# The first norm of a transformer step in four K quarters, each followed by that quarter of three column blocks of the first FFN

## The reference

```
mod = silu(cond) @ ada_w + ada_b           # nine vectors of 2048: shift, scale, gate for each of three norms
h   = rms_norm(x, norm_w) * (1 + scale) + shift
g,u = split(h @ wi)                        # wi is 2048 x 11264, wo is 5632 x 2048
x   = x + 0.5 * gate * ((silu(g) * u) @ wo)
```

## Time and profile before

| | |
|---|---|
| median of three runs | 2425.38 us |
| the profiled execution: its span | 2427.3 us (the page gives no other time of it) |
| PE busy | 2315.6 us, 95% |
| DVE, ACT busy | 1249.6 us, 931.9 us |
| HBM read | 543.73 MB, 225 GB/s over the span |

### The profile page before, as it was taken

One profiled execution on the slowest core, in us unless ns is written; L12 is line 12 of the kernel. 1 busy time (PEld: TensorE's weight loads), 2 busy tenths in 40 slices (PEclk: granted clock), 3 DMA queues, 4 the chain that ended last, 5 costly groups with the idle time before them and its releaser, 6 DMA issues.

```text
span 2427.3 us, 29221 instructions
## 1 busy us (share of the span) xinstructions
PE 2315.6 (95%) x11108; PEld 1798.5 (74%) x11108; DVE 1249.6 (51%) x1289; ACT 931.9 (38%) x1083; POOL 59.9 (2%) x57
## 2 busy tenths in 40 slices
PE   5699999999999998999977999998999999999998
PEld 0277777777777776777766888787888888888886
DVE  1154455554555547444457455455455555555557
ACT  0253333333333334433445344345434444444442
POOL 0000000000000000000040000000000000000000
PEclk7699999999999998999989999999999999999999
DMA  9969788787787875789611555655555555555553
GB/s 367 330 215 323 253 285 284 253 310 264 280 289 251 304 272 191 277 297 321 231 50 42 185 193 181 202 196 175 186 196 190 190 194 190 189 190 189 191 190 112
DMA packets 273183, 547.86 MB, mean 226 GB/s; under 512 B 9022, under 2 KB 9190, under 8 KB 272880
## 3 DMA queue, kind: packets, MB, share of 16 engines
q1 hardware_dynamic: 193936, 386.36, 46.8%
q10 hardware_dynamic: 76176, 151.15, 17.2%
q0 software_dynamic: 3024, 9.71, 1.4%
HBM read 543.73 MB, written 3.46 MB: 225 GB/s over the span
## 4 chain that ended last, share of the span: by engine, by line
PE 91%; DMA 4%; DVE 3%; ACT 1%; issue 0%; ACTq 0%; DVEq 0%
PE ps L525 27%; PE ps L527 27%; PE ps L526 27%; PE ps L486 5%; DMA ada_w_sb<-in_ada_w 4%; PE ps L512 1%; PE ps L600 1%; DVE w_lo L1145 0%; PE ps L496 0%; ACTq L896 0%; PE ps L749 0%; DVE x L1276 0%; DVE acc L1274 0%; PE ps L834 0%; PE ps L730 0%
## 5 line engine op out<-in xcount | busy, mean ns | idle before, releaser
L1145 DVE TENSOR_TENSOR w_lo<-raw_w,w_hi 128x1024 fp32r<-128x1024 f32 x728 | 895.6, 1231 | 898.6 <-ACT w_hi L885 898.1
L885 ACT CAST w_hi<-raw_w 128x1024 fp32r<-128x1024 f32 x728 | 765.5, 1053 | 1246.1 <-PE ps L527 1210.5
L525 PE MATMUL ps<-w_hi,xT_hi 128*128 128x512 f32 x2080 | 823.1, 396 | 5.1 <-DVE xT_lo L1201 2.6
L527 PE MATMUL ps<-w_hi,xT_lo 128*128 128x512 f32 x2080 | 811.2, 390 | 0.0
L526 PE MATMUL ps<-w_lo,xT_hi 128*128 128x512 f32 x2080 | 811.0, 390 | 0.0
L525 PEld LDWEIGHTS ps<-w_hi,xT_hi 128*128 128x128 f32 x2080 | 391.3, 188 | 115.7 <-issue 29.3
L527 PEld LDWEIGHTS ps<-w_hi,xT_lo 128*128 128x128 f32 x2080 | 391.1, 188 | 83.0
L526 PEld LDWEIGHTS ps<-w_lo,xT_hi 128*128 128x128 f32 x2080 | 391.6, 188 | 77.5
L525 PE MATMUL ps<-w_hi,hT_hi 128*128 128x512 f32 x704 | 276.4, 393 | 5.6 <-DVE hT_lo L1215 5.6
L527 PE MATMUL ps<-w_hi,hT_lo 128*128 128x512 f32 x704 | 275.4, 391 | 0.0
L526 PE MATMUL ps<-w_lo,hT_hi 128*128 128x512 f32 x704 | 275.1, 391 | 0.0
(11 more groups left out here) (225 smaller groups left out, 867.1 us busy)
## 6 DMA issues: line engine op xcount, KB each, us to landing
raw_w<-in_ffn_wi SPq DMA_DIRECT2D x176, 1024.0 KB, 5.1
ada_w_sb<-in_ada_w ACTq DMA_DIRECT2D x144, 1024.0 KB, 9.5
raw_w<-in_ffn_wo SPq DMA_DIRECT2D x88, 1024.0 KB, 5.0
raw_w<-in_w_in SPq DMA_DIRECT2D x68, 1024.0 KB, 5.3
raw_w<-in_w_out SPq DMA_DIRECT2D x16, 1024.0 KB, 5.1
raw_w<-in_w_proj_m SPq DMA_DIRECT2D x8, 1024.0 KB, 5.0
raw_w<-in_w_proj_a SPq DMA_DIRECT2D x8, 1024.0 KB, 5.1
gate_bc<-gate_dram POOLq DMA_DIRECT2D x6, 1024.0 KB, 9.6
```

The source lines that it names most:

```text
L525: pe.matmul(out, a_hi, w_hi[:, slot, kk, :], start=(first and kk == 0), stop=False)
L527: mm = pe.matmul(out, a_lo, w_hi[:, slot, kk, :], start=False, stop=(last and kk == 1))
L885: act.copy(w_hi[:, us % SPL, :, :], raw_w[:, slot, 2 * half:2 * half + 2, :]).then_inc(hi_ready, 1)
L1145: dve.tensor_tensor(w_lo[:, us % SPL, :, :], raw_w[:, slot, 2 * half:2 * half + 2, :], w_hi[:, us % SPL, :, :].bitcast(F32), ALU.subtract) ...
```

## The change

The eight chunks of SH1 and SC1 are taken in pairs, scale and shift of the same 512 rows of K (`PRE_CHUNKS`). SP now issues them, each pair followed by three raw tiles. ACT issues the constants, and x once the first tile is used. The norm matmuls are done with the first two chunks, and their results are copied from PSUM to `xm` (`xn_copy`). Then come four quarters. In each, `norm0_quarter` modulates 512 rows of K in SBUF and splits them, and six units (`QT`) follow: g of block 0, u of block 0 and g of block 1, two units each, into banks 0 to 5. The tiles of the next pair of chunks are used between these units: one after each of units 1, 2 and 3, the other five ahead of unit 4. In the last quarter two tiles of chunk 8 take that place. `second` does what is left until iteration 2: the 8 units of u of block 1 with chunks 8 and 9, and the output product of block 0. The loop of the first FFN starts at 2. Semaphore counts of later norms are shifted. The diff, cut to its core (SP, PE, ACT, DVE in that order):

```diff
 ADA_PRE = 8
+PRE_CHUNKS = [v * 4 + q for q in range(4) for v in (SC1, SH1)] + [4 * G1]
+QT = 6
...
-            sp.dma_start(cst[:], I["consts"]).then_inc(cst_landed, 16)
-            for n, name in enumerate(("c_ctx", "c", "norm_ffn1_w", "norm_mix_w", "norm_ffn2_w")):
...
-            sp.wait_ge(ada_used, 8)
-            sp.dma_start(x[:, CTX, :], I["x_prompt"][0]).then_inc(x_landed, 16)
-            sp.dma_start(x[:, LAT, :], I["x_sample"][0]).then_inc(x_landed, 16)
-            sp.wait_ge(ada_used, 4 * ADA_PRE - 4)
+            def ada_load(n, tiles=range(4)):
+
+                c = PRE_CHUNKS[n]
+                if 0 in tiles:
+                    at_least(sp, ada_rows_done, n - 1)
+                    src = I["ada_b"][0:1, c * CH:(c + 1) * CH].broadcast_to([GROUPS, CH])
+                    sp.dma_start(ada_bias[0:GROUPS, n % 2, :], src).then_inc(bias_landed[n % 2], 16)
+                for q in tiles:
+                    w = I["ada_w"][0].rearrange("(q k p) n -> q p k n", k=4, p=P)[q]
+                    at_least(sp, ada_used, 4 * n + q - 3)
+                    sp.dma_start(ada_w_sb[:, q, :, :], w[:, :, c * CH:(c + 1) * CH]).then_inc(ada_landed[q], 16)
...
+                if f == 0:
+                    sp.wait_ge(bias_zeroed, 1)
+                    for q in range(4):
+                        ada_load(2 * q)
+                        ada_load(2 * q + 1)
+                        for n, col in enumerate((0, D_FF, CH)):
+                            tile(t0 + 3 * q + n, 0, rows(wi, q)[:, :, col:col + CH])
+                    for q in range(4):
+                        if q < 2:
+                            ada_load(ADA_PRE, (2 * q, 2 * q + 1))
+                        tile(t0 + 12 + q, 0, rows(wi, q)[:, :, CH + D_FF:2 * CH + D_FF])
+                    ffn_out(0, t0 + 16, 0)
...
+            def ada_q(c, q):
+                if q == 0:
+                    at_least(pe, ada_rows_done, c)
+                pe.wait_ge(ada_landed[q], 16 * (c + 1))
+                for j in range(4):
+                    mm = pe.matmul(ps[32 * j:32 * j + 32, 6, :], ctile[:, 4 * q + j, :],
+                                   ada_w_sb[:, q, j, :], start=(q == 0), stop=(q == 3))
+                mm.then_inc(ada_used, 1)
...
+                def prologue():
+                    for q in range(4):
+                        a, b = 2 * q + 2, 2 * q + 3
+                        for m in range(QT):
+                            if q < 3 and m == 4:
+                                ada_q(a, 3)
+                                ada_sel(a)
+                                ada_q(b, 0)
+                                ada_T(a)
+                                for r in range(1, 4):
+                                    ada_q(b, r)
+                            if q < 3 and m == 5:
+                                ada_sel(b)
+                            kb = 4 * q + 2 * (m % 2)
+                            pe.wait_ge(xT_lo_ready, kb // 2 + 1)
+                            unit(u0 + QT * q + m, 0, xT_hi, xT_lo, kb, 2 * (m // 2), kb == 0, kb == KD - 2)
+                            if q == 0 and m == 1:
+                                pe.wait_ge(xn_dve, 4)
+                            if q == 0 and m == 3:
+                                pe.wait_ge(xn_act, 4)
+                            if q < 3 and 1 <= m <= 3:
+                                ada_q(a, m - 1)
+                            if q == 3 and m >= 4:
+                                ada_q(ADA_PRE, m - 4)
+                        if q < 3:
+                            ada_T(b)
+                def second():
+                    def u_between(k):
+                        if k < 2:
+                            ada_q(ADA_PRE, k + 2)
+                        if k == 1:
+                            pe.wait_ge(silu_done, 2)
+                            h_transposes(0)
...
+                    pe.wait_ge(h_done, 1)
+                    x_chunk(u0 + 24, 0, 2, u_between)
+                    ffn_out(0, u0 + 32, 0, between=out_between)
+                    h_transposes(1)
...
-            for c in range(ADA_PRE):
-                ada_acc(c)
-                ada_sel(c)
-                ada_T(c)
-                if c == 5:
-                    norm(0, range(6))
-            pe.wait_ge(ada_cols_done, ADA_PRE)
-            norm(0, range(6, 8))
+            ada_acc(0)
+            ada_sel(0)
+            ada_T(0)
+            for q in range(2):
+                ada_q(1, q)
+            norm(0, range(4))
+            for q in range(2, 4):
+                ada_q(1, q)
+            ada_sel(1)
+            norm(0, range(4, 6))
+            ada_T(1)
+            norm(0, range(6, 7))
+            pe.wait_ge(ada_cols_done, 2)
+            norm(0, range(7, 8))
...
+            def norm0_quarter(q):
+                def hi(j):
+                    act.copy(xT_hi[:, 2 * j:2 * j + 2, :], xm[:, 2 * j:2 * j + 2, :]).then_inc(xT_hi_ready, 1)
+                split(QT * q, 0)
+                act.wait_ge(acol_ready, q + 1)
+                act.wait_ge(xn_act, q + 1)
+                for b in range(2):
+                    for g in range(GROUPS):
+                        k = 4 * q + 2 + b
+                        ins = act.activation(xm[:, k, g * P:(g + 1) * P], xm[:, k, g * P:(g + 1) * P], ACT.Identity,
+                                             scale=acol[:, k, g:g + 1], bias=adacols[:, SH1 * KD + k, g:g + 1])
+                ins.then_inc(xm_act, 1)
+                act.wait_ge(xm_ready, q + 1)
+                hi(2 * q)
+                act.wait_ge(xm_act, q + 1)
+                hi(2 * q + 1)
+                split(QT * q + 1, 0)
...
+                def prologue():
+                    for q in range(4):
+                        norm0_quarter(q)
+                        if q == 0:
+                            xn_copy(3)
+                        for m in range(2, QT):
+                            split(u0 + QT * q + m, 0)
+                    act.wait_ge(units_done, u0 + 20)
+                    act.activation(sg[:], ps[:, 0:2, :], ACT.Silu).then_inc(silu_done, 1)
...
-            act.wait_ge(bias_zeroed, 1)
-            ada_load(0, 0)
+            act.dma_start(cst[:], I["consts"]).then_inc(cst_landed, 16)
+            for n, name in enumerate(("c_ctx", "c", "norm_ffn1_w", "norm_mix_w", "norm_ffn2_w")):
...
+            act.wait_ge(ctile_zeroed, 1)
             act.activation(ctile[:, :, 0:GROUPS].rearrange("p k g -> p g k"),
                            ps[:, 0, 0:GROUPS * KD].rearrange("p (g k) -> p g k", g=GROUPS),
                            ACT.Silu).then_inc(cond_silu, 1)
-            for c in range(1, 6):
-                ada_load(c, c % 2)
+            act.wait_ge(ada_used, 1)
+            act.dma_start(x[:, CTX, :], I["x_prompt"][0]).then_inc(x_landed, 16)
+            act.dma_start(x[:, LAT, :], I["x_sample"][0]).then_inc(x_landed, 16)
             act.wait_ge(x_landed, 32)
             for n in range(NCH):
                 sumsq(0, n)
             root(0)
-            for c in range(6, ADA_PRE):
-                ada_load(c, c % 2)
-            for u in range(AHEAD):
-                split(u, 0)
-            ada_load(ADA_PRE, 0)
-            norm(0, SH1)
+            def xn_copy(n):
+                j = 2 * n + 1
+                act.wait_ge(norm_ps, j + 1)
+                act.copy(xm[:, 2 * j:2 * j + 2, :].rearrange("p a t -> p (a t)"), ps[:, j, :]).then_inc(xn_act, 1)
+            for n in range(3):
+                xn_copy(n)
...
+            def xn_copy(n):
+                j = 2 * n
+                dve.wait_ge(norm_ps, j + 1)
+                dve.tensor_copy(xm[:, 2 * j:2 * j + 2, :].rearrange("p a t -> p (a t)"), ps[:, j, :]).then_inc(xn_dve, 1)
+            def low(j, at):
+                dve.wait_ge(xT_hi_ready, at)
+                dve.tensor_tensor(xT_lo[:, 2 * j:2 * j + 2, :], xm[:, 2 * j:2 * j + 2, :],
+                                  xT_hi[:, 2 * j:2 * j + 2, :].bitcast(F32), ALU.subtract).then_inc(xT_lo_ready, 1)
+            def norm0_quarter(q):
+                ks = slice(4 * q, 4 * q + 4)
+                dve.wait_ge(ada_cols_done, 2 * q + 2)
+                dve.scalar_tensor_tensor(
+                    acol[:, ks, :], adacols[:, SC1 * KD + 4 * q:SC1 * KD + 4 * q + 4, :], 1.0,
+                    normw[:, 0, ks].unsqueeze(2).to_broadcast([P, 4, GROUPS]), ALU.add, ALU.mult).then_inc(acol_ready, 1)
+                dve.wait_ge(acol_ready, q + 1)
+                dve.wait_ge(xn_dve, q + 1)
+                for b in range(2):
+                    for g in range(GROUPS):
+                        k = 4 * q + b
+                        ins = dve.tensor_scalar(xm[:, k, g * P:(g + 1) * P], xm[:, k, g * P:(g + 1) * P],
+                                                acol[:, k, g:g + 1], adacols[:, SH1 * KD + k, g:g + 1], ALU.mult, ALU.add)
+                ins.then_inc(xm_ready, 1)
+                split(QT * q, 0)
+                low(2 * q, 2 * q + 1)
+                dve.wait_ge(xm_act, q + 1)
```

(79 more changed lines are left out.)

83 lines of the change are left out of this document (58 added, 25 removed).

## The result

The changed kernel takes 2407.97 us (median of four runs, 2406.15 to 2409.77) against 2424.8 for the kernel before (median of four runs here): a ratio of 0.9929, 95% interval 0.9915 to 0.9943, so 14 to 21 us less. Measured a second time, beside the experiments, its ratio was 0.9920 (0.9906 to 0.9934). Forecast were 22.5 us less, 2403, with a range of 2392 to 2416.

A forecast was written before the change was run, and what follows sets the result against it. TensorE was taken as the bound, except where modulation weights are awaited. First unit 46.5, three quarters of 34.7, then the rest put iteration 2 at 225.0, 22.5 us less: 2425.4 - 22.5 = 2403, range 2392 to 2416.

The forecast's parts named there:

- The whole question is when iteration 2 starts: First FFN: later iterations stay at 75.40 us, so only the start of iteration 2, 247.53 before, matters.
- If anything shifts behind iteration 2: After iteration 2 starts: a sign that the prediction is wrong, as only numbering changes there.
- First unit at 46.5: Start of the first quarter: after loads, norm, transposition and modulation, the first unit begins at 46.5 us.
- A quarter of 34.7: Each quarter before the last: 32.2 of work and waits, plus clock dips of 1.5 at start and 1.0 in the middle.
- From the last quarter to iteration 2, 74.4 with the switches: Last quarter's start at 150.6 to iteration 2 at 225.0: 19.6, then 53.6, and 1.2 for switches.
- Sum 225.0 for iteration 2: Start of iteration 2 in the first FFN: 225.0 us against 247.53 before, 22.5 less.
- 2425.4 - 22.5: Whole kernel: the median before, less the gain at iteration 2, gives 2403 us.
- SP isn't held by the raw tiles; POOL's loads cost nothing; DVE keeps up: In the quarters: raw-tile slots are free a quarter earlier, POOL's loads cost nothing (-1 to +3), DVE's splits nothing.
- More hidden (0.10): Rival, chance 0.10: the quarters' middle waits and their clock dips vanish, 13 us more gained, 2390.
- A hungrier quarter: Rival, chance 0.15: single tiles land in 9.0 us, not 5.1, so quarters' middles grow; 13 us lost, 2416.
- The clock stays down: Rival, chance 0.03: clock at 0.50 throughout the quarters' work, 72 us lost, 2475.
- It doesn't overlap: Rival, chance 0.02: SP held until a quarter's units are done, 46.9 us a quarter instead of 34.7, 2440.

The follow-up runs named there:

- mid_early: Changed kernel with the four tiles of each pair's first chunk used one place earlier: 2395.47 us, ratio 0.9869 to the kernel before.
- serial_stream: Kernel before, no quarters: SP issues the eight chunks, ACT constants and x, x after first tile's use, norm banks spread: 2417.42 us against 2426.23, ratio 0.9961.
- light_after: Changed kernel with only 256 KB of 1 MB loaded for each of raw tiles 4 to 11: ratio 0.9924 to the kernel before.

## Why the prediction was right, and where it was off

Step by step, in the changed kernel's trace:

- *The whole question is when iteration 2 starts.* Right: 19.9 of 21.5 us between the spans were won by then. "If anything shifts behind iteration 2" came true by 1.6 us, far behind the change; a level of the clock is part of it, the rest is open.
- *First unit at 46.5.* 45.95, and 44.94 in the second profile, with norm matmuls at 29.99 for 30.1. In part this was luck. The first modulation matmul came at 9.09, not 7.8: the start lost 0.6 us where 0.7 gained was written, since the PE waited for the small loads (`colrows`) until 8.41, and until 4.87 in the kernel before. So x was asked for at 11.09 instead of 9.8, but its halves landed in 7.9 and 10.7 us, not 9.0 and 11.9, and ACT began on it at 22.27 for 22.1.
- *A quarter of 34.7.* 36.3, 35.05 and 36.45. The waits, read from the second quarter, were about right: 0.81 for 0.9, 2.74 for 2.4, a bubble of 3.38 for 3.8, since modulation out of SBUF took 1.11 for the 1.4 assumed. The dip at the start was 1.6 for 1.5, at all four starts; in the second profile the first start had none. In the middle two of three quarters had one, 1.0 on average as taken. **The term that was mis-sized is the PE's work besides the units: the 8 tiles, 7.3 us, with selections and transpositions, 1.5.** I had priced a tile at 0.91 out of groups of four back to back (3.57 for 32 records). A lone tile takes 1.06, and with the switches around it the unit stream loses 1.2: 53.03, when the next matmul was due, to 54.12, and 0.1 more on the matmul behind. In the second quarter, 35.05 less 6.93 of waits and 1.6 of clock leave 26.5 of work where I had 25.1. Of these 1.4 the two lone tiles are 0.6, and the rest are switches around the other tiles and selections. Three quarters make 4, of which the 1.2 for switches at the end of my sum had covered a part.
- *From the last quarter to iteration 2, 74.4 with the switches.* 153.77 to 227.6, 73.8.
- *Sum 225.0 for iteration 2.* 227.6, in the second profile about 225.7 (2.9 ahead of chunk 10).
- *2425.4 - 22.5.* Measured are 16.8 and 20.4 us by the medians of the two measurements. Of the 5.7 that the first is short, 2.6 are the sum's. The rest is the base: the sum was laid against the trace of an execution that was some 4 us slower than its fellows, by the estimate above, while the 22.5 were taken from their median.
- *SP isn't held by the raw tiles; POOL's loads cost nothing; DVE keeps up.* Right: no wait of the PE between 43 and 230 us but for low parts of x, ada_w and bias additions.
- *More hidden (0.10).* Not what the change does, but what it leaves: mid_early makes a good part of it true by one edit of the order, with 3.4 us of waits for ada_w left.
- *A hungrier quarter.* It did not come: the two waits are 1.09 and 1.65 for 0.7 and 1.7.
- *The clock stays down.* It did not: 0.93 on average from 50 to 170 us.
- *It doesn't overlap.* It does: the DMA share from 45 to 154 us is 0.88; 0.85 was written.

What the prediction had wrong in its reasons and not in its number: it gave the gain to the 18 units laid into the stream. serial_stream gets half of it with none of them laid so, out of the pauses that the start of the kernel before had. Shown is that the clean stream alone gives 9.9 us at iteration 2 and the whole change 19.9. That the other 10 are the quarters' is the difference of the two, each from one profile, and not a run of its own.

## What to carry to other kernels

When work is laid between arrivals, write the timetable of each buffer: when it is asked for, when given back, when the next transfer can be issued. Here, with the same transfers, 12 us more were gained by the medians (7 at iteration 2) when tiles were used one unit earlier, so that buffers came free earlier and a bias addition was covered. Covering a chain of small steps with one unit gained 12 by itself (5 at iteration 2). With both, one quarter ran into the full stream. Before crediting an overlap, try the version that only removes the pauses of the stream, and price a small matmul group as it will stand, alone between others, not as it stood in a row.

## What was not expected of the hardware

The issue of a DMA can itself be slow: that of the 4 KB bias took SP 0.36 us at 1.98 us, ahead of all tiles, and 2.50 at 102.75, with the tiles of a quarter ahead of it. The timeline of SP in the changed kernel:

```profile
1.98 0.36 SPq L311 DMA_DIRECT2D ada_bias<-in_ada_b  x1
...
99.83 2.88 SPq L320 DMA_DIRECT2D raw_w<-in_ffn_wi  x3
102.75 2.50 SPq L311 DMA_DIRECT2D ada_bias<-in_ada_b  x1
```

light_after shows that it goes with what was asked for ahead of it. At the same place, behind three raw tiles of 256 KB instead of 1 MB, the issue took 0.32 us:

```profile
97.87 0.32 SPq L311 DMA_DIRECT2D ada_bias<-in_ada_b  x1
```

It cost nothing here, as SP has no other work; that on ACT the casts would have stood behind it no run shows.

And the same wait of 1.65 us was followed by a dip of the clock in two quarters of the changed kernel and not in the third, in both of its profiles. That may be part of why its runs spread over 2402.65 to 2410.94 us in its second measurement; it isn't shown.
